# A hybrid decoder block in fp32r on one core: another matmul order and other tile addresses where 272 columns move

## The reference

```python
hs = concatenate([meta, x], axis=1)                       # (1, 272, 2048)
hs = hs + 0.5 * swiglu(rmsnorm(hs, ffn1_norm), w_gate, w_up, w_down)      # d_ff = 5632
hs = hs + token_mixing(rmsnorm(hs, mix_norm), ...)
hs = hs + 0.5 * swiglu(rmsnorm(hs, ffn2_norm), ...)       # same shapes as the first
out = rmsnorm(hs, final_norm)[:, 16:]

def token_mixing(h, ...):
    u = h @ w_in + b_in                                   # 2048 -> 5 x 1024: b, c, v, a, g
    y_sc = b * causal_dwconv(c * v, conv_sc_w)            # 3 taps
    z = causal_dwconv(a * sigmoid(g), conv_cf_w) + conv_cf_b     # 31 taps
    y_cf = silu(layernorm(z, ln_cf_g, ln_cf_b))
    return concatenate([y_sc, y_cf], axis=-1) @ w_out
```

## Time and profile before

| | |
|---|---|
| median of 3 runs | 1861.69 us (1861.58 to 1861.81) |
| profiled execution | 1861.53 us, of it 1859.7 us span |
| granted TensorE clock | 0.999 of full speed, mean |
| PE busy | 99% of the span, 14425 matmuls |
| VectorE / ScalarE busy | 59% / 49% |
| DMA | 342.29 MB, mean 184 GB/s |

### The profile page before, as it was taken

The page is one execution under the profiler, slowest core; times in us unless marked ns, Lnnn a source line. Parts: engine busy times, 40 slices in busy tenths (PEclk is TensorE's granted clock), DMA queues, the critical chain, the costliest instruction groups (busy, mean ns, idle before and its releaser), DMA issues.

```text
span 1859.7 us, 34886 instructions
## 1 busy us (share of the span) xinstructions
PE 1848.6 (99%) x14425; PEld 1803.6 (97%) x14425; DVE 1088.2 (59%) x1218; ACT 902.5 (49%) x1151; POOL 5.8 (0%) x16
## 2 busy tenths in 40 slices
PE   9999999999999999999999999999999999999998
PEld 9999999999999999999999999999999999988886
DVE  7555555555554544469899887555555555544454
ACT  6433333434343444359888665444444444444443
POOL 1000000000000000000000000000000000000000
PEclk9999999999999999999999999999999999999999
DMA  6655555555555555555555566666666666656664
GB/s 224 192 178 172 180 171 179 172 177 174 176 176 176 180 174 179 180 170 173 182 182 172 179 201 193 196 192 193 193 194 193 195 193 193 214 188 191 193 188 134
DMA packets 283359, 342.29 MB, mean 184 GB/s; under 512 B 10639, under 2 KB 223985, under 8 KB 283152
## 3 DMA queue, kind: packets, MB, share of 16 engines
q1 hardware_dynamic: 282672, 340.44, 58.3%
q10 hardware_dynamic: 320, 0.53, 0.1%
q0 software_dynamic: 288, 0.19, 0.0%
HBM read 339.02 MB, written 2.10 MB: 183 GB/s over the span
## 4 chain that ended last, share of the span: by engine, by line
PE 99%; DVE 1%; ACT 0%; issue 0%; DVEq 0%
PE ps L484 29%; PE ps L482 28%; PE ps L483 28%; PE ps L578 4%; PE ps L576 4%; PE ps L577 4%; PE ps L464 0%; DVE w_flat_lo L889 0%; PE ps L444 0%; PE ps L594 0%; DVE zc L1090 0%; PE ps L601 0%; DVE ln_mu L915 0%; PE ps L498 0%; ACT o_tok L874 0%; DVE res L1004 0%
## 5 line engine op out<-in xcount | busy, mean ns | idle before, releaser
L889 DVE TENSOR_TENSOR w_flat_lo<-raw,w_flat_hi 128x1024 fp32r<-128x1024 f32 x296 | 361.7, 1224 | 325.8 <-ACT w_flat_hi L661 325.7
L661 ACT ACTIVATE w_flat_hi<-raw 128x1024 fp32r<-128x1024 f32 x296 | 313.9, 1061 | 428.0 <-PE ps L484 286.2
L484 PE MATMUL ps<-x_hi,w_rows_lo 128*128 128x272 f32 x1664 | 483.3, 290 | 0.0
L482 PE MATMUL ps<-x_hi,w_rows_hi 128*128 128x272 f32 x1664 | 479.8, 288 | 1.3 <-DVE x_lo L898 1.2
L483 PE MATMUL ps<-x_lo,w_rows_hi 128*128 128x272 f32 x1664 | 472.3, 284 | 0.0
L889 DVE TENSOR_TENSOR w_rows_lo<-raw,w_rows_hi 128x1024 fp32r<-128x1024 f32 x207 | 253.3, 1224 | 238.0 <-ACT w_rows_hi L661 237.3
L482 PE MATMUL ps<-x_hi,w_flat_hi 128*128 128x256 f32 x1408 | 388.7, 276 | 0.1
L483 PE MATMUL ps<-x_lo,w_flat_hi 128*128 128x256 f32 x1408 | 388.6, 276 | 0.0
L484 PE MATMUL ps<-x_hi,w_flat_lo 128*128 128x256 f32 x1408 | 388.6, 276 | 0.0
L661 ACT ACTIVATE w_rows_hi<-raw 128x1024 fp32r<-128x1024 f32 x207 | 218.9, 1059 | 313.8 <-PE ps L484 312.5
L483 PEld LDWEIGHTS ps<-x_lo,w_rows_hi 128*128 128x128 f32 x1664 | 317.5, 191 | 0.0
(11 more groups left out here) (164 smaller groups left out, 2524.0 us busy)
## 6 DMA issues: line engine op xcount, KB each, us to landing
raw<-in_ffn_w_up SPq DMA_DIRECT2D x176, 512.0 KB, 3.5
raw<-in_ffn_w_down SPq DMA_DIRECT2D x176, 512.0 KB, 4.6
raw<-in_ffn_w_gate SPq DMA_DIRECT2D x175, 512.0 KB, 3.5
raw<-in_w_in SPq DMA_DIRECT2D x80, 512.0 KB, 3.5
raw<-in_w_out SPq DMA_DIRECT2D x32, 512.0 KB, 4.8
x_tok<-in_x SPq DMA_DIRECT2D x4, 512.0 KB, 7.7
gain_tok<-in_final_norm SPq DMA_DIRECT2D x1, 1024.0 KB, 5.0
out_y<-o_tok SPq DMA_DIRECT2D x2, 512.0 KB, 2.9
```

Source lines behind the costliest of these rows:

```text
L482: pe.matmul(dst, w_high, act_high, start=first, stop=False)
L484: return pe.matmul(dst, w_low, act_high, start=False, stop=last)
L661: act.activation(w_of[phase][0][s], raw_rows(phase, s), ACT.Copy).then_inc(hi_ready, 1)
L889: dve.tensor_tensor(w_lo, raw_rows(phase, s), w_hi.bitcast(F32), ALU.subtract).then_inc(lo_ready, 1)
```

## The change

gu1 and ag (but for the first group of gu1) and down1 get a new order. For each of a block's two column tiles, `row_blocks` does all four row blocks of the first of the three products, then all four of the second, then of the third: 12 matmuls into one bank, each moving another row than the one ahead of it. down1 now loads blocks of four row blocks by 256 columns, columns 0 to 255 and 256 to 511 of its group in turn, and has a function of its own. cv and gu2 put the column tile outside and the row block inside, and so do b and both outs; they keep the three matmuls of `product` together. x and a start at 0 modulo 256 instead of 192; x2 and y, which lie in the same regions, are moved so that they still start at 192, and a2 at 0. `w_rows` serves gu1, ag and down1, cv takes the packed `w_flat4` and b the packed `w_flat2`.

```diff
-        sb("to_rows", [P, (192 - nc.sbuf_base) % 256 // 32 * 8])
+        sb("to_rows", [P, (0 - nc.sbuf_base) % 256 // 32 * 8])
...
+        sb("to_w", [P, -nc.sbuf_base % 256 // 32 * 8])
...
-        assert w_at % 256 == 0 and x_at % 256 == a_at % 256 == 192 and 4 * BUFFER % 256 == 0
+        assert w_at % 256 == 0 and x_at % 256 == a_at % 256 == 0 and 4 * BUFFER % 256 == 0
...
-        x2_hi = at("x2_hi", x_at + 0, [P, KD, SEQ], F32R)
-        x2_lo = at("x2_lo", x_at + 0 + 4 * KD * SEQ, [P, KD, SEQ], F32R)
+        x2_hi = at("x2_hi", x_at + 192, [P, KD, SEQ], F32R)
+        x2_lo = at("x2_lo", x_at + 192 + 4 * KD * SEQ, [P, KD, SEQ], F32R)
...
-        w_of = {"gu1": w_rows, "ag": w_rows, "cv": w_near, "down1": w_pairs, "b": w_kept,
+        w_of = {"gu1": w_rows, "ag": w_rows, "cv": w_flat4, "down1": w_rows, "b": w_flat2,
...
-        a2_both = at("a2_both", a_at + 64, [P, 2, KF, SEQ], F32R)
+        a2_both = at("a2_both", a_at + 0, [P, 2, KF, SEQ], F32R)
...
-        mix_at = a_at + 0
+        mix_at = a_at + 192
...
-            single("down1", ffn1_w_down[0], 0)
+            paired("down1", ffn1_w_down[0], ffn1_w_down[0], 0, 256, 512)
...
+            def row_blocks(bank, w_high, w_low, cols, act_high, act_low, k, first, last):
+
+                for q, (w, act) in enumerate(((w_high, act_high), (w_high, act_low), (w_low, act_high))):
+                    for c in range(4):
+                        m = pe.matmul(ps[:, bank, 0:T], w[:, c, cols], act[:, k + c, :],
+                                      start=first and q == 0 and c == 0, stop=last and q == 2 and c == 3)
+                return m
...
-                        for j, c in [(j, c) for c in range(4) for j in range(2)]:
+                        if phase in ("gu1", "ag") and not opening:
+                            k = 4 * (i // 2)
+                            if norm and first_group and i % 2 == 0:
+                                pe.wait_ge(xlo_ready[norm], k + 4)
+                            for j in range(2):
+                                m = row_blocks(SET * parity + 2 * (i % 2) + j, w_hi, w_lo, slice(j * P, (j + 1) * P),
+                                               x_hi, x_lo, k, k == 0, k + 4 == KD)
+                        for j, c in ([(j, c) for c in range(4) for j in range(2)] if opening else
+                                     [(j, c) for j in range(2) for c in range(4)] if phase in ("cv", "gu2") else []):
...
+            def down_group(g):
+
+                start_group("down1", g)
+                for i in range(N_DOWN):
+                    w_hi, w_lo = (w[slot("down1", g, i)] for w in w_of["down1"])
+                    start_block("down1", g, i)
+                    k = 4 * (i // 2)
+                    if g == 0:
+                        pe.wait_ge(alo_ready["gu1"], k // 2 + 2)
+                    for j in range(2):
+                        m = row_blocks(SET * (g % 2) + 2 * (i % 2) + j, w_hi, w_lo, slice(j * P, (j + 1) * P),
+                                       a1_hi, a1_lo, k, k == 0, k + 4 == KF)
+                    m.then_inc(block_used, 1)
...
-                    for c in range(2):
-                        k = 2 * i + c
-                        for j in range(SET):
-                            cols = slice(j * P, (j + 1) * P)
+                    for j in range(SET):
+                        cols = slice(j * P, (j + 1) * P)
+                        for c in range(2):
+                            k = 2 * i + c
...
-                single_group("down1", g, g % 2, a1_hi, a1_lo, 0, ALL, KF, alo_ready["gu1"], lambda i: i + 1)
+                down_group(g)
```

More of the change, by code:

```diff
@@ L135, in build @@
         w_rows = weights("w_rows", 4, ROW_BLOCK, lambda s: 0)
-        w_near = weights("w_near", 4, ROW_BLOCK, lambda s: 4 * (T - NEAR))
-        w_pairs = weights("w_pairs", 2, BANK + META, lambda s: 128 * (s % 2))
-        w_kept = weights("w_kept", 2, BANK + META, lambda s: 128 * (s % 2) + 4 * META)
         w_flat4 = weights("w_flat4", 4, 256, lambda s: 0)
         w_flat2 = weights("w_flat2", 2, BANK, lambda s: 0)
-        w_of = {"gu1": w_rows, "ag": w_rows, "cv": w_near, "down1": w_pairs, "b": w_kept,
+        w_of = {"gu1": w_rows, "ag": w_rows, "cv": w_flat4, "down1": w_rows, "b": w_flat2,
                 "out_sc": w_flat2, "out_cf": w_flat2, "gu2": w_flat4, "down2": w_flat2}
@@ L359, in load, with paired @@
                 sp.dma_start(raw[s][:, :].rearrange("p (c n) -> p c n", n=n), src).then_inc(raw_loaded[s], 16)
-            def paired(phase, wa, wb, col_a, col_b):
+            def paired(phase, wa, wb, col_a, col_b, per_group=256):
                 rows = [w.rearrange("(q c p) n -> q p c n", c=4, p=P) for w in (wa, wb)]
@@ L369, in body @@
                                 load_x(q)
-                        src = rows[i % 2][i // 2, :, :, bass.ds(g * 256 + (col_a, col_b)[i % 2], 256)]
+                        src = rows[i % 2][i // 2, :, :, bass.ds(g * per_group + (col_a, col_b)[i % 2], 256)]
                         if phase == "gu1" and isinstance(g, int) and g == 0 and i == 0:
```

## The result

The changed kernel takes 1870.69 us (1870.53 to 1870.86) against 1861.69: a ratio of 1.0048, 95% interval 1.0034 to 1.0063. It is slower by 9.0 us, where the prediction had 1833.5 and a range up to 1865. The profiled execution has a span of 1868.7 us, 9.0 more than before.

What follows compares the result with a forecast made beforehand. PE's matmul spacing was taken as the bound: gu1 −17.3, ag −3.3 and down1 −7.6 sum to −28.2 us, all else 0, giving a median of 1833.5 us; likeliest case 1825 to 1840, 8 in 10 from 1827 to 1865.

Steps and rivals of the forecast that it cites:

- What bounds the kernel: Whole kernel: TensorE (PE) busy 1848.6 of 1859.7 us, loads and splits ahead, so time is matmuls times their spacing.
- By 0.4427 ns a column, 272 columns should take 120.4 ns: gu1, ag, down1: spacing in proportion to columns; gu1 and ag pay 4.3 ns over 120.4, down1 3.6.
- rival 1: gu1, ag, down1: each change of moving row costs 8.3 ns; new order +49 us, 1911; chance 0.14.
- jump back: gu1 before: the next matmul restarts at the same row address, five times of six; said to explain 123.3 above 120.4.
- So both relations of gu2 hold at every matmul: New gu1, ag, down1: each row starts where the last ended, next tile 64 ahead; −28.2 us together.
- Rival 2: gu1, ag, down1: the 272-column stream locks at 120.4 + 4.6 = 125.0 ns; 1865 us; chance 0.07.
- as I read from out_sc: out_sc: 17 matmuls with unchanged tile layout at 117.6 ns, the stage beside at 113.3: two steady paces.
- Rival 3: All stages: place and order do not matter, spacing is set by the columns; nothing moves, 1861.7 us; chance 0.06.
- cv, b and out_sc: Bounds cv −4.4 to +3.0 us, b −1.8 to +1.0, out_sc 0.9 saved to 2.7 lost; each taken as 0.
- gu2 stayed at 113.3: gu2: start addresses stay, only order changes, taken as 0; falling to its other pace would cost +19.4 us.
- loads, waits and VectorE: down1's loads, waits in down1 and ag, VectorE in the mixing part: each 0; uncovered loads could cost down1 7.6 us.
- The starts that I gave for down1 and ag: Sign of a right prediction: down1 starts near 522 and ag near 776 us.

Runs made afterwards that it cites:

- 0, 1, 3, 2 with rows at 0: Changed kernel with row_blocks taking the last two row blocks swapped, x and a still at 0: 1868.91 us, ratio 1.0039 to the kernel before.
- 0, 1, 3, 2 with rows at 64: Changed kernel with the last two row blocks swapped and x and a at 64 modulo 256: 1852.94 us, ratio 0.9953 to the kernel before.

## Why the prediction was wrong

- *What bounds the kernel* was right: PE's spacing is the time, before and after, and 8.9 of the 9.0 us are found in it.
- *"By 0.4427 ns a column, 272 columns should take 120.4 ns"* is the step that failed. The proportion came from 256 and 512 columns alone and does not hold at 264, 272, 288 or 304. Of the 37 us between 1833.5 and 1870.7, 6912 × 2.9 = 20 are of this step (123.3 for 120.4); the next one has 6912 × 2.8 = 19 (126.1 for 123.3) and with it the sign; 2 came back in cv, b and out_sc. Over some 150 stretches of 272 columns, and every stage of every kernel, the lowest steady pace was 123.3. At that pace gu1, ag and down1 gain 4800 × 1.4 + 2112 × 0.7 = 8.2 us, not 28.2, and no order that was tried gives more. The number was in my working: rival 1 solved for a base of 123.3 between changes of row, and I explained it away as a jump back.
- *"So both relations of gu2 hold at every matmul"* was right as arithmetic and wrong as a cause. The new order has both, no jump and the tile 64 ahead, and runs at 125.8 or 126.1. Rows of 272 columns on a pitch of 1280, all at 192, keep only the second, since each ends 64 past the next one's start (modulo 256), and run at 123.3. The two relations do not set the pace.
- *Rival 2, the other steady pace,* was nearest in number, with 125.0 and 1865, off by 1.1 ns. That is in part luck: it was built as 120.4 + 4.6, and there is no 120.4. I gave it 0.07. That several paces exist for one sequence, as I read from out_sc, was right. But for the order of the change a fast one never appeared, in 13 stretches.
- *Rival 1, a price per change of row,* had the right sign and fell on its mechanism: with fixed starts a new row at every matmul costs nothing (12.12 against 12.11 us a stretch), and 126.1 is far from its 131.6. What its arithmetic fitted is the step of the start in the old order: 123.3 with fixed starts, 124.6 ascending.
- *Rival 3* fell: starts alone move 256 columns from 113.3 or 117.8 (rows at 192) to 119.8 (rows at 0). I had put it beside the Trainium skill's rule ("TensorE: Matmul & The Clock Gate", "Step-by-step: what each phase is for"), that loading weights takes nothing from the running matmul. The stream moves although no other engine works; whether it is the weight load that takes something, no run shows.
- *cv, b and out_sc,* taken as 0, gave −1.3, −0.2 and −0.7, inside their bounds. gu2 stayed at 113.3, and loads, waits and VectorE cost nothing, as forecast. The starts that I gave for down1 and ag, 522 and 776, don't follow from my sum, which has 523.8 and 778.2.

## What to carry to other kernels

Before a layout or an order is built on a lowest price per column, measure that price at the width that is used: 256 columns don't tell what 264 or 272 cost. Where PE runs without a gap, a kernel that does nothing but the matmul stream tries 60 layouts in one run and here gave a stage's spacing to within 0.3 ns, unless the sequence has more than one pace (0, 1, 3, 2 with rows at 0: 123.4 in the probe, 125.8 in the kernel). So enter each candidate several times, and choose one that finds its fast pace every time (here 0, 1, 3, 2 with rows at 64, six of six), not one that found it once.

## What the runs showed of the hardware

- One sequence of matmuls can have several steady paces, and keeps the one it settles on: 123.3 or 125.8 ns for one sequence of 272 columns, 113.3 or 117.8 for one of 256, in probes and in whole stages. Whether what ran ahead picks the pace or chance does was not separated. The times of one program, too, lie in two groups: the kernel with rows from last to first has times near 1857.3 and 1859.6 us, and the kernel before, run beside it 15 times, has twelve from 1861.3 to 1862.1 and three from 1863.8 to 1864.2.
- From 208 to 240 columns a matmul cost about the same, 10.97 to 11.02 us a stretch of 96, some 111.7 ns; from 256 to 264 columns the cost rises by 6.7 ns. By the Trainium skill ("TensorE: Matmul & The Clock Gate", section "LDWEIGHTS (loading the stationary operand)") loading a tile takes P / 1.2, with 128 columns 107 ns, an estimate. The floor in these stretches lies near it, 5 ns higher; whether the load sets it, no run shows.
- What in the chip ties the spacing to starts, and what picks one pace of several, stays open: the runs give the map, not the mechanism.
